# The order of three products in the down projections: low weights first for one token half, and turned about for the other

## The reference

```python
o = jnp.concatenate([o_n, o_m], axis=-1) @ w_o[l]
...
f = jnp.square(jax.nn.relu(h @ w_up[l])) @ w_down[l]
x = x + gate_f[:, None, :] * rms_norm(f, post_norm_ffn[l])
```

## Time and profile before

| | |
|---|---|
| median of 3 runs | 2958.71 us (2955.77 to 2965.56) |
| the profiled execution | 2959.03 us, span 2957.2 us |
| TensorE matmuls busy | 2869.5 us, 97% |
| TensorE weight loads busy | 2646.1 us, 89% |
| VectorE busy | 1701.3 us, 58% |
| ScalarE busy | 1254.1 us, 42% |
| mean granted TensorE clock | 0.985 of 2.4 GHz |

### The profile page before, as it was taken

One profiled execution on the slowest core, in us unless ns is written; L12 is line 12 of the kernel. 1 busy time (PEld: TensorE's weight loads), 2 busy tenths in 40 slices (PEclk: granted clock), 3 DMA queues, 4 the chain that ended last, 5 costly groups with the idle time before them and its releaser, 6 DMA issues.

```text
span 2957.2 us, 50977 instructions
## 1 busy us (share of the span) xinstructions
PE 2869.5 (97%) x22328; PEld 2646.1 (89%) x22328; DVE 1701.3 (58%) x1507; ACT 1254.1 (42%) x1197; POOL 135.4 (5%) x111
## 2 busy tenths in 40 slices
PE   6898999999999999999999999999999999999998
PEld 5898987799889997899999889999979998899887
DVE  7879887795444454455455654445745554455444
ACT  3334444444334543345343544443345443344333
POOL 0011120000000000000022320000000000000000
PEclk8799999999999999999999999999999999999999
DMA  9999778596556665555442015566554555565553
GB/s 358 386 317 308 265 235 299 171 366 228 194 188 197 190 194 184 196 189 181 161 165 68 10 45 197 188 198 218 181 185 158 198 186 198 187 197 189 181 194 119
DMA packets 300452, 596.72 MB, mean 202 GB/s; under 512 B 12144, under 2 KB 17776, under 8 KB 299760
## 3 DMA queue, kind: packets, MB, share of 16 engines
q1 hardware_dynamic: 294864, 587.83, 58.9%
q10 hardware_dynamic: 5408, 6.23, 0.8%
HBM read 583.80 MB, written 6.29 MB: 200 GB/s over the span
## 4 chain that ended last, share of the span: by engine, by line
PE 84%; DVE 8%; DMA 3%; ACT 3%; issue 2%; POOL 0%; SPq 0%; ACTq 0%; DVEq 0%
PE ps L2431 30%; PE ps L2354 26%; PE ps L2958 9%; PE ps L2538 4%; PE ps L2553 3%; DVE ada_acc L1593 2%; DVE wL L1373 2%; PE ps L3081 2%; DMA ada<-w_ada 2%; PE ps L2839 2%; ACT wH L770 1%; PE ps L2512 1%; DMA raw<-w_up 1%; PE ps L2377 1%; PE ps L2333 0%
## 5 line engine op out<-in xcount | busy, mean ns | idle before, releaser
L1373 DVE TENSOR_TENSOR wL<-raw,wH 128x2048 fp32r<-128x2048 f32 x436 | 1005.4, 2306 | 1062.4 <-ACT wH L770 1058.1
L770 ACT ACTIVATE wH<-raw 128x2048 fp32r<-128x2048 f32 x436 | 837.8, 1921 | 1277.8 <-PE ps L2431 467.7
L2431 PE MATMUL ps<-actH,wH 128*128 128x256 f32 x2816 | 779.5, 277 | 1.7 <-DVE wL L1373 1.6
L2431 PE MATMUL ps<-actL,wH 128*128 128x256 f32 x2816 | 777.8, 276 | 0.0
L2431 PE MATMUL ps<-actH,wL 128*128 128x256 f32 x2816 | 777.8, 276 | 0.0
L2431 PEld LDWEIGHTS ps<-actH,wH 128*128 128x128 f32 x2816 | 529.1, 188 | 4.2 <-DVE wL L1373 2.1
L2431 PEld LDWEIGHTS ps<-actL,wH 128*128 128x128 f32 x2816 | 529.1, 188 | 0.1
L2431 PEld LDWEIGHTS ps<-actH,wL 128*128 128x128 f32 x2816 | 529.0, 188 | 0.0
L2354 PE MATMUL ps<-wH,hidH 128*128 128x512 f32 x1024 | 403.4, 394 | 1.3 <-DVE wL L1373 1.3
L2354 PE MATMUL ps<-wH,hidL 128*128 128x512 f32 x1024 | 400.4, 391 | 0.0
L2354 PE MATMUL ps<-wL,hidH 128*128 128x512 f32 x1024 | 397.4, 388 | 0.0
(11 more groups left out here) (438 smaller groups left out, 3652.4 us busy)
## 6 DMA issues: line engine op xcount, KB each, us to landing
raw<-w_in SPq DMA_DIRECT2D x96, 1024.0 KB, 5.2
ada<-w_ada SPq DMA_DIRECT2D x80, 1024.0 KB, 8.2
raw<-w_up SPq DMA_DIRECT2D x64, 1024.0 KB, 5.3
raw<-w_down SPq DMA_DIRECT2D x64, 1024.0 KB, 5.2
raw<-w_mlp_up SPq DMA_DIRECT2D x64, 1024.0 KB, 5.2
raw<-w_mlp_down SPq DMA_DIRECT2D x64, 1024.0 KB, 5.0
raw<-w_gates SPq DMA_DIRECT2D x48, 1024.0 KB, 5.1
raw<-w_o SPq DMA_DIRECT2D x16, 1024.0 KB, 6.0
```

Of the source, the lines that this page charges most:

```text
L770: nc.scalar.activation(wH[:, s % SPLIT if L[name]["spg"] > 1 else r % SPLIT, :, :], raw[:, slot, :, :], ACT.Copy).then_inc(wh_ready, 1)
L1373: nc.vector.tensor_tensor(wL[:, b, :, :], raw[:, slot, :, :], wH[:, b, :, :].bitcast(F32), ALU.subtract).then_inc(wl_ready, 1)
L2431: ins = nc.tensor.matmul(out, w[:, b, k, cols], v[:, kk, :], start=(kk == 0 and j == 0 and n % 2 == 0), stop=(kk == STEP_K * spg - 1 and j ...
```

## The change

In `layer_t` alone, the three products of a row tile stand in another order. For the first token half the product with the low weights comes first; for the second half the list is turned about, so that its product with the low weights comes last. The sums are the same but for the order of addition.

```diff
                             for t in range(TT):
                                 ts = slice(t * P, (t + 1) * P)
-                                for j, (v, w) in enumerate(((xH, wH), (xH, wL), (xL, wH))):
+                                products = (xH, wL), (xH, wH), (xL, wH)
+                                for j, (v, w) in enumerate(products[::-1] if t else products):
                                     ins = nc.tensor.matmul(ps[:, acc(name, r) + t, :], v[:, kk, ts], w[:, b, k, :],
                                                            start=(kk == 0 and j == 0), stop=(kk == STEP_K * spg - 1 and j == 2),
                                                            skip_group_check=True)
```

## The result

The changed kernel takes 2977.09 us (median of 6 runs, 2972.32 to 2980.61) against 2960.38 us of the kernel before (6 runs, 2955.77 to 2965.56): a ratio of 1.0052, 95% interval [1.0036, 1.0069]. It is slower, by about 17 us, and lies above the predicted range.

A forecast was written before the change was run, and what follows sets the result against it. TensorE's unbroken matmul streams were taken to bound the kernel. Counts 0, waits 0, switches 0 and pairing +3.1 us summed to +3.1 us on 2959.03 us: about 2962 us, range 2949 to 2974, within 0.3% likeliest (0.64).

The forecast's parts named there:

- What bounds the kernel: TensorE's unbroken matmul streams bound it, 97% busy; the edited line holds 26% of the span; clock and DMA no bound.
- counts: On the edited line all 3,456 matmuls stay, each with its own weight load: 0 us.
- waits: Reading wL first in a step of 24 matmuls asks for nothing sooner, and buffers are released as before: 0 us.
- Switches of the moving tile: Within a row tile, switches between wH and wL fall from four to two; claimed to gain 0 us.
- the 15.6 ns over the bare stream: Excess of the 228.9 ns pitch over 213.3 ns for 512 columns; if all switches and half went, 27 us gained.
- The pairing with the next load: Hidden stages: four of six moving streams overlap a load from a tile placed unlike; 1.5 ns each, +3.1 us.
- the nearest row: The output projection w_out2, stationary tiles without offset: pitch 230.4 ns, 1.5 ns more, taken as the price of unlike pairs.
- my upper bound of 14.3: Most the pairing could cost in us: 7 ns for four in six of 3,072 matmuls, from w_out2's longest duration.
- The rival that named the pairing: Slower by unlike pairs in the hidden stages: at 7 ns each 2973 us; chance 0.22.
- The 216 ns: The skill's N/2.4 + 2.5 ns for a warm stream of 512 columns; the trace shows 228.9 ns.
- that piece is 179 us or more: Sign of a wrong forecast: first long piece of 768 matmuls this long means pairing costs over 4 ns.
- Durations that wander: Sign of the pairing term: first piece at 176.6 us, its matmul durations no longer standing at one value.

The follow-up runs named there:

- e7: Changed kernel with LOW_AT = 64 instead of 192 (wL and hidL 128 bytes lower): first piece of 768 matmuls 178.46 us, ratio 1.0128.
- e8: Kernel before with LOW_AT = 64 instead of 192 (wL and hidL 128 bytes lower): first piece of 768 matmuls 178.45 us, ratio 1.0124.
- e3: Kernel before with hidH and hidL at their base addresses, without any offset: first piece of 768 matmuls 176.93 us, pitch 230.4 ns.
- e4: Changed kernel with hidH and hidL at their base addresses, without any offset: first piece of 768 matmuls 176.64 us, pitch 230.0 ns.
- e2: Changed kernel with hidH and hidL 128 bytes lower: first piece of 768 matmuls 177.52 us, pitch 231.1 ns.
- e6: Kernel before with only the turn added, its order mirrored in the second token half: first piece of 768 matmuls 176.64 us, pitch 230.0 ns.
- e5: Changed kernel without the turn, low weights first in both token halves: first piece of 768 matmuls 176.81 us, pitch 230.2 ns.
- e1: Kernel before with hidH and hidL 128 bytes lower: first piece of 768 matmuls 177.50 us, pitch 231.1 ns.
- e11: Changed kernel with the two token halves' orders exchanged: first piece of 768 matmuls 177.49 us; the two second pieces of 624 took 144.47 and 146.53 us.
- e15: The kernel of e11 again, unchanged, timed in rounds against the kernel before: ratio 1.0042; its first piece of 624 matmuls took 146.53 us.
- e13: Changed kernel with the first row tile of each group in the order of before: piece of 768 as expected, 180.0 us, to 0.05 us.
- e14: Kernel before with the first row tile of each group in the changed order: piece of 768 as expected, 175.9 us, to 0.05 us.

## Why the prediction was wrong

*What bounds the kernel, counts, waits*: right. TensorE's unbroken pieces took all of the change, the counts and the 1.00 clock are the same, and reading `wL` first in a step made nobody wait.

*Switches of the moving tile*: 0 was right as far as it can be seen (e7 and e8, the same placement with two switches and with four, took 178.46 and 178.45 us). Where the switches fell from four to two and the placement was plain, the pitch fell by 0.4 ns (e3 to e4, and `w_out2` from 77.43 to 77.30 us); had the 15.6 ns over the bare stream been paid at switches, half of it would have gone.

*The pairing with the next load*: this is the step that failed: "I take the mean of the nearest row, 1.5 ns for four in six: 1.5 x 2,048 = 3.1 us". It measured 17.0 us, above even my upper bound of 14.3, which I had from the longest duration in `w_out2`. The nearest row was another placement in the order of before, and says little of another order. The rival that named the pairing gave the right sign, and its price of 7 ns an unlike pair would have to be 8.3 by the result. But its mechanism was wrong, so sign and size came by luck. No price for each unlike pair fits: none unlike gives 228.9 (before) or 232.4 (e7, e8), two give 231.1 (e2) or 230.0 (e6), four give 234.4 (after) or 230.2 (e5), six give 231.1 (e1), and within the changed kernel the longest gap, 240.9 ns, is at a like pair. What the runs showed in its place is that order and placement act together: the same order loses 5.5 ns in the places written, and nothing in three others (e2, e4, e7).

*By the Trainium skill* (TensorE: Matmul & The Clock Gate, "What happens when you issue a matmul") the load of the next tile takes no read bandwidth from the running matmul. By that placement should cost nothing, and the runs disagree: e1 and e3 change only where the stationary tiles lie, and the matmuls start 2.2 and 1.5 ns further apart. Whether it is read bandwidth that is lost, or something else, no run shows. The 216 ns that the prediction took from the same page's "Back-to-back issue gap" is called there the gap of isolated matmuls; no term of the sum used it.

*The signs named beforehand*: "that piece is 179 us or more" was the one that came. Durations that wander came too, and `w_out2` and the up projection stayed as forecast. The matmuls of the first piece after the change, by kind, with minimum, median and maximum in ns:

```profile
L2355 PE MATMUL ps<-wL,hidH x255: 388/397/399, 740.7 to 919.3; 128*128 128x512 f32 x128
L2355 PE MATMUL ps<-wH,hidH x255: 392/399/404, 740.9 to 919.6; 128*128 128x512 f32 x128
L2355 PE MATMUL ps<-wH,hidL x255: 389/396/398, 741.2 to 919.8; 128*128 128x512 f32 x128
```

Here each kind has a spread of 9 to 12 ns, where in the earlier trace rows each stood at one value.

What is shown: the pitch of the stream depends on the order of the six products together with the places of the operand tiles; the changed order in the places written runs at 234.4 ns, and neither that order (e4: 230.0) nor those places (before: 228.9) do so alone. Also shown is that the stream repeats a fixed pattern of gaps, and that one ring of tiles can have two such patterns. Argued only: that the two streams collide at some resource in SBUF. Which resource, what picks the pattern, and whether the changed order could also run in the faster one (231.1 ns, 3.3 of the 5.5 lost), stays open.

## What to carry to other kernels

In a stage where matmuls follow each other without a wait, read the pitch (a piece of the chain divided by its count) and not the durations or waits: an edit that changes no count and no wait can still cost 2% of the stage. Order and placement of operand tiles are tuned together; if one is changed, try the other again before dropping it, since the same order was 5.5 ns worse in one placement, 0.4 ns better in another and equal in two. For the price of a stream that the trace doesn't hold, a nearby row is no bound: measure the stream.

## What the runs showed of the hardware

A dense stream of matmuls can have two steady paces for one code and one set of addresses: 113.3 or 117.8 ns with 256 columns in e7 (174.09 and 180.91 us for 1,536), and 231.5 or 234.8 ns with 512 columns in e11 (144.47 and 146.53 us for 624). Each holds for the whole unbroken piece. In e15 the piece that had the faster pace in e11 had the slower. The steady paces in e11 are 231.1 and 234.4 ns once the entry is left out, each with its own pattern of six gaps. The pieces of the kernel before all keep one pace, and so do those of the changed one, even with a disturbed entry (e13, e14). So a layout should be judged by whether its pieces agree with each other, too.

The place of the longest gap in the slow pattern, 240.9 ns, also has the longest load beside it: the load for the first of the two wL,hidH takes 192 ns there, in the changed kernel as in the slow piece of e11, and 188 ns in e11's fast pieces, like all the others (187 or 188). So at the place where that pattern loses most, a load is slower too.
